# The fifth block of head 1, transposed by itself between the projection products

## The reference

```python
h = rmsnorm(x, g_pre_mix)
proj = h @ w_in + b_in             # split into queries, keys, values of two groups
out_a = mixer_a(...)               # group A: 8 query heads, 2 key heads, window of 128, sinks
out_b = mixer_b(...)               # group B: 8 heads of 64, own chunk of 64 and 8 chunks to the left
y = concat(out_a, out_b) @ w_out
x = x + rmsnorm(y, g_post_mix)
u = square(relu(rmsnorm(x, g_pre_mlp) @ w_up))
x = x + rmsnorm(u @ w_down, g_post_mlp)
```

## Time and profile before

| | us |
|---|---|
| median of 3 runs | 1027.13 (1026.74 to 1027.49) |
| the profiled execution | 1027.07 |
| its span, first to last instruction | 1025.3 |
| TensorE busy in the span | 1016.1 (99%) |
| VectorE busy | 767.8 (75%) |
| ScalarE busy | 476.8 (47%) |
| GpSimd busy | 220.0 (21%) |

### The profile page before, as it was taken

One profiled execution on the slowest core, in us unless ns is written; L12 is line 12 of the kernel. 1 busy time (PEld: TensorE's weight loads), 2 busy tenths in 40 slices (PEclk: granted clock), 3 DMA queues, 4 the chain that ended last, 5 costly groups with the idle time before them and its releaser, 6 DMA issues.

```text
span 1025.3 us, 15760 instructions
## 1 busy us (share of the span) xinstructions
PE 1016.1 (99%) x5458; PEld 844.1 (82%) x5458; DVE 767.8 (75%) x1498; ACT 476.8 (47%) x990; POOL 220.0 (21%) x218
## 2 busy tenths in 40 slices
PE   9999999999999999999999999999999999999997
PEld 8899887777778888888888888888888888888886
DVE  4954678767787668888988777776454877778997
ACT  6622355656577568745311311311344444454562
POOL 5200000000000003168765765762100000000000
PEclk9999999999999999999999999999999999999999
DMA  9935442232171563046444344347777733464344
GB/s 200 229 97 134 109 127 70 84 112 82 50 227 42 164 186 124 21 165 226 175 156 149 148 163 152 141 160 234 233 247 240 226 93 100 136 197 142 93 139 171
DMA packets 145312, 152.32 MB, mean 149 GB/s; under 512 B 76984, under 2 KB 95680, under 8 KB 143184
## 3 DMA queue, kind: packets, MB, share of 16 engines
q1 hardware_dynamic: 144160, 151.08, 47.3%
q10 hardware_dynamic: 688, 0.20, 0.1%
q0 software_dynamic: 384, 0.04, 0.0%
HBM read 103.65 MB, written 47.49 MB: 147 GB/s over the span
## 4 chain that ended last, share of the span: by engine, by line
PE 95%; issue 2%; DVE 2%; ACT 1%; DMA 0%; DVEq 0%; SPq 0%; ACTq 0%
PE ps L2336 28%; PE ps L2338 28%; PE ps L2337 28%; PE ps L2565 2%; PE ps L2528 2%; PE ps L2547 2%; PE ps L2470 1%; PE ps L2505 1%; PE ps L2682 1%; PE ps L2684 1%; PE ps L2670 1%; DVE wc_lo L2012 1%; DMA xraw<-in_x 0%; ACT prob_b L1244 0%; PE ps L2700 0%
## 5 line engine op out<-in xcount | busy, mean ns | idle before, releaser
L2336 PE MATMUL ps<-b_hi,wc_hi 128*128 128x512 f32 x448 | 174.6, 390 | 0.2 <-DVE wc_lo L2012 0.2
L2337 PE MATMUL ps<-tm_lo,sm_hi 128*128 128x512 f32 (+1 forms) x450 | 174.6, 388 | 0.0
L2338 PE MATMUL ps<-tm_hi,sm_lo 128*128 128x512 f32 (+1 forms) x450 | 174.6, 388 | 0.0
L2336 PE MATMUL ps<-tm_hi,sm_hi 128*128 128x512 f32 (+1 forms) x450 | 174.6, 388 | 0.0
L2338 PE MATMUL ps<-b_hi,wc_lo 128*128 128x512 f32 x448 | 174.3, 389 | 0.0
L2337 PE MATMUL ps<-b_lo,wc_hi 128*128 128x512 f32 x448 | 174.3, 389 | 0.0
L1561 ACT ACTIVATE sm_hi<-sm_raw 128x512 fp32r<-128x512 f32 x112 | 70.7, 631 | 162.3 <-DMA sm_raw<-u_matrices 162.3
L2240 DVE TENSOR_TENSOR sm_lo<-sm_raw,sm_hi 128x512 fp32r<-128x512 f32 x112 | 78.1, 697 | 77.4 <-ACT sm_hi L1561 76.9
L2336 PEld LDWEIGHTS ps<-b_hi,wc_hi 128*128 128x128 f32 x448 | 84.1, 188 | 18.1 <-DVE wc_lo L2012 0.6
L2338 PEld LDWEIGHTS ps<-tm_hi,sm_lo 128*128 128x128 f32 x450 | 84.5, 188 | 17.5
L2336 PEld LDWEIGHTS ps<-tm_hi,sm_hi 128*128 128x128 f32 x450 | 84.5, 188 | 17.5
(11 more groups left out here) (266 smaller groups left out, 2053.5 us busy)
## 6 DMA issues: line engine op xcount, KB each, us to landing
u_matrices<-stage SPq DMA_DIRECT2D x112, 256.0 KB, 2.0
sm_raw<-u_matrices SPq DMA_DIRECT2D x112, 256.0 KB, 2.6
up_raw<-in_w_up SPq DMA_DIRECT2D x16, 1024.0 KB, 5.0
w<-in_w_down SPq DMA_DIRECT2D x64, 256.0 KB, 3.7
w_raw<-in_w_in SPq DMA_DIRECT2D x8, 512.0 KB, 3.7
xr<-in_x SPq DMA_DIRECT2D x8, 512.0 KB, 4.2
x_rows<-xr SPq DMA_DIRECT2D x8, 512.0 KB, 4.9
xf<-x_rows SPq DMA_DIRECT2D x8, 512.0 KB, 3.5
```

What stands on the lines that cost most here:

```text
L2336: pe.matmul(out, w_hi_, x_hi_, start=start, stop=False)
L2337: pe.matmul(out, w_hi_, x_lo_, start=False, stop=False)
L2338: return pe.matmul(out, w_lo_, x_hi_, start=False, stop=stop)
```

## The change

The fifth block of head 1 of steps 36 to 39 and 44 to 47 is no longer transposed together with the other four ahead of the fills. It is transposed by itself between the second and the third fill of the same pass, and into bank 6, the bank of the other four. Its former chunk is therefore the first chunk of the same step, and the first chunk's former is the fifth block of the step before. Steps with fewer key blocks and the steps that are not turned keep their order and their banks.

```diff
@@ chunk_banks
             elif turned_b(n):
-                bank = 5 if paired(n) and n % T == 1 else (6, 5)[c]
+                bank = 5 if paired(n) and n % T == 1 else 6
@@ TensorE's loop over the steps of group B
                 elif not paired(n - 1):
-                    for c in range(min(2, len(chunks_of(n - 1)))):
+                    for c in range(1 if turned_b(n - 1) else 2):
                         transposes(n - 1, c)
                 for m in range(first, end):
                     if m == first + 3 and n % T == 3:
                         transposes(n, 0)
-                    elif m == first + 2 and len(chunks_of(n - 1)) == 3:
-                        transposes(n - 1, 2)
+                    elif m == first + 2 and keys_of(n - 1) == B_KEYS:
+                        transposes(n - 1, len(chunks_of(n - 1)) - 1)
                     fill(m)
```

## The result

The changed kernel takes 1029.93 us (median of 11 runs, 1029.6 to 1030.3), the kernel before on the same chip 1027.35 (11 runs): the ratio is 1.0026, with a 95% interval of 1.0018 to 1.0034. The profiled span grew from 1025.3 to 1028.1 us.

The account below looks back on a forecast made before the run. TensorE was taken to bound the kernel, with 95% of the chain. A 1.98 us stall, partly given back, leaves 1.46 us in each of two head pairs: 1027.1 + 2.9 = 1030.0 us, range 1028.9 to 1031.5.

Parts of the forecast that it names:

- The stall: Pass 37: the lone transpose waits for ScalarE's copy, 200.52 instead of 198.54, 1.98 us; scores of step 38 2.04 late.
- What pass 38 gives back: First fill of step 38 at 203.63, 1.35 us late, without the wait for `tmp`; 0.7 us comes back.
- the drain of 0.2 to 0.3 us: Step 38: time from the end of the scores' last product until VectorE can start on them, at 203.4 to 203.5.
- The lone transpose at zero: Changed steps: the single transpose costs 0.11 us, just what the group ahead saves, hence zero per step.
- Passes 38 to 40: No stall: 0.5 us to spare at 38, 0.25 at 39; the delay leaves these steps as 1.46 us.
- The second head pair: Same rows 40.93 us later, transposes at 237.59, copy at 240.74: another 1.46 us.
- the rival that put 0.9 us there: Waits of the last attention steps on ScalarE and VectorE swallow up to 0.9 us: 1029.1 us, chance 7%.
- The clock: Rival, chance 3%: a 2 us pause brings products to 1.2 GHz, fills take 2.8 us more, twice; about 1036 us.
- the fifth block's copy frees the bank long before it is wanted: Step 38: VectorE's copy of the single block, ahead of `tmp`, frees the bank long before the transposes at 203.22.

Follow-up runs that it names:

- the third experiment: Changed kernel, but in passes 37 and 45 ScalarE copies the first chunk before its two exponentials: 1027.65 us, ratio 1.0004.
- the fourth: Changed kernel with the lone transpose one fill later, ahead of the fourth fill instead of the third: 1029.04 us, ratio 1.0016.
- the fifth experiment: Changed kernel with the lone transpose in bank 5 and VectorE reading the finished fill half in passes 37 and 45, not 38 and 46: 1026.91 us, ratio 0.9996.
- the first experiment: Changed kernel with only the bank undone, the fifth block still transposed alone but into bank 5: 1027.69 us, ratio 1.0002.
- the second experiment: Kernel before with only the bank changed, all five transposes ahead of the fills, the fifth into bank 6: 1041.04 us (four runs), ratio 1.0135.
- sixth: Kernel before, five transposes together, with VectorE reading the finished fill half in passes 37 and 45, not 38 and 46: 1027.50 us, ratio 1.0003.

## Why the prediction was right

It gave 1030.0 us and +2.9; the medians say 1029.93 and +2.6, the spans +2.8. By its steps:

- *The stall.* Forecast: the transpose at 200.52, scores of step 38 at 202.14. Measured: 200.49 and 202.12. Two small misses cancel in the start: the copy ended 0.04 us later than forecast (200.43), and the transpose followed it after 0.06 us and not 0.13. As the trace counts idle time the waits are 1.68 and 1.74 us, where about 1.9 was written. That ScalarE's order makes the stall, the third experiment shows by taking it away with nothing else changed; that its length is copy end less place, the fourth shows by moving the place.
- *What pass 38 gives back.* Forecast: first fill at 203.63, no wait for `tmp`. Measured: 203.61 and none. The kernel before spent this time waiting for `tmp` and in a longer group of transposes ahead of it, and in the trace of the fifth experiment, where `tmp` comes earlier, the wait is gone too. One estimate on this path was right without its reason: the drain of 0.2 to 0.3 us was taken from products said to overlap by 0.39 us, but 0.39 is a product's duration, and 0.23 from start to start leaves an overlap of 0.16. VectorE began all the same 0.25 us after the scores' end on TensorE (203.45 against 203.20).
- *The lone transpose at zero.* Between the products of pass 39 its slot is 0.03 us at the next start and 0.09 at the one after, 0.12 where 0.11 was taken; the first experiment has no loss to show. The Trainium skill (TensorE: Matmul & The Clock Gate, Part 4) gives about 275 ns for a bf16 transpose in one kernel. The lone float32 transpose here lasts 0.27 us as well, but that is its duration and not its slot.
- *Passes 38 to 40.* Forecast: no stall, the copy of pass 39 ending 0.38 us ahead of the transpose's place (0.25 with the release taken off). Measured: no stall; it ended 0.51 us ahead. Such a margin is thin: in the third experiment an exchange for which VectorE waited 0.72 us was enough for a wait of 0.22 us at this place.
- *The second head pair* waited 1.74 us where the first waited 1.68. The end of attention (the first low product of the output projection) came at 322.8 against 319.8 us, so nothing was given back in the last attention steps; the rival that put 0.9 us there falls.
- *The clock.* It stayed at 1.00 through both pauses, and none of the 11 runs has a mean clock under 0.998. The rival was wrong for this change, but its 3% rested on no row: nothing in the kernel before showed what a pause of 2 us does, and the second experiment shows the low clock one us of waiting further on. In this the forecast had luck.

One thing was argued too simply: that the fifth block's copy frees the bank long before it is wanted. That holds only because TensorE comes late. With the stall gone, in the third experiment, there is a wait of 0.42 us there.

## What to carry to other kernels

When work is moved into a gap of the bounding engine, ask for each of its operands and for its target buffer who releases it and what stands ahead of that in the releaser's queue: here the copy was 0.58 us of work, and 2 us late because two exponentials stood ahead of it, which nobody had reason to mind. A shared buffer makes its reader's late copy a bound on the next writer; here either its own bank for the fifth block, or the copy moved into ScalarE's idle time, took the loss away. What such a stall costs is its length less the waits just behind it that it covers, so read the next pass before multiplying.

## What the runs showed of the hardware

A pause of TensorE can cost more than its length. Pauses of 1.68 and 1.74 us (some 2 us from the last product to the transpose) left the granted clock at 1.00. In the second experiment it read 0.56 in the 5 us around the end of a pause of 2.74 us, and the products of 512 columns behind it came 0.43 us apart, the 1.2 GHz level, instead of 0.23. The Trainium skill (TensorE: Matmul & The Clock Gate, Part 1) states that idling throttles the clock to that level, and the trace of this experiment agrees. The length of the pause alone does not set the cost: behind 3.14 us the clock fell only after some five products, and took 1.5 us where it took 2.5 behind the shorter pause. What else decides it, no run here shows; an earlier wait of 1.20 us, 9 us ahead of the shorter pause's end, may have had a part.

The exchange of head 0 by DMA adds a scatter of its own. In pass 38 VectorE waited 0.72 to 0.77 us for `turn_in` in the profiled executions of the first, third and sixth experiments, and not at all in the kernel before or in the changed one. In that of the second it waited 2.07 us in pass 36, ahead of anything the edit touches, and TensorE lost 1.20 there.
